# A two-layer fp32 transformer block: which engine empties the banks of interleaved work, and where modulation units of layer 0 stand

## The reference

```python
for layer in range(DEPTH):
    need_ctx = layer < DEPTH - 1
    mod_l = [m[:, None, :] for m in adaln_params(c, w_mod[layer], b_mod[layer])]   # silu(c) @ w_mod + b_mod, in 6
    mod_c = adaln_params(c_ctx, w_mod[layer], b_mod[layer])
    p_l = split_cols(modulate(x, norm1_g[layer], mod_l[0], mod_l[1]) @ w_in[layer])
    p_c = split_cols(modulate(ctx, norm1_g[layer], mod_c[0], mod_c[1]) @ w_in[layer])
    a_l, a_c = diff_attention(...)       # "DA": two softmaxes and their difference
    b_l, b_c = hgrn2_mixer(...)          # "HG": gated recurrence in both directions
    n_l, n_c = neighbourhood_attention(...)
    w_l, w_c = window_gqa(...)
    x = x + mod_l[2] * (jnp.concatenate([a_l, b_l, n_l, w_l], axis=-1) @ w_out[layer])
    x = x + mod_l[5] * squared_relu_mlp(modulate(x, norm2_g[layer], mod_l[3], mod_l[4]), w_ff1[layer], w_ff2[layer])
```

## Time and profile before

| | |
|---|---|
| median of 3 runs | 2276.91 us (2276.86 to 2279.08) |
| the profiled execution | 2280.41 us, its span 2278.6 us |
| mean granted clock of TensorE | 0.959 of full |
| busy, share of the span | TensorE 91%, VectorE 45%, ScalarE 34%, GpSimd 30% |
| DA in layer 0 / layer 1 | 377 to 496 us / 1594 to 1680 us |
| HG's levels in layer 0 / layer 1 | 568.3 to 661.3 us / 1737 to 1805.2 us |

### The profile page before, as it was taken

One profiled execution on the slowest core, in us unless ns is written; L12 is line 12 of the kernel. 1 busy time (PEld: TensorE's weight loads), 2 busy tenths in 40 slices (PEclk: granted clock), 3 DMA queues, 4 the chain that ended last, 5 costly groups with the idle time before them and its releaser, 6 DMA issues.

```text
span 2278.6 us, 32056 instructions
## 1 busy us (share of the span) xinstructions
PE 2083.6 (91%) x13292; PEld 1734.6 (76%) x13292; DVE 1017.8 (45%) x1791; ACT 784.8 (34%) x1283; POOL 686.2 (30%) x567
## 2 busy tenths in 40 slices
PE   5799898889889899999999988998998888999998
PEld 3578787768777788888888867777787677778787
DVE  2535546855775631212213253445857754121122
ACT  1533323434335621312213153233444355232231
POOL 0230212012751232322322323223024513444442
PEclk9889998989999999999999998999999989999999
DMA  8220010342411121121121123010242311222222
GB/s 287 48 74 19 20 38 19 130 138 83 149 57 56 38 74 56 56 75 56 56 74 56 56 46 76 19 38 19 93 119 93 112 56 56 93 93 93 94 91 74
DMA packets 178353, 169.72 MB, mean 74 GB/s; under 512 B 29393, under 2 KB 174753, under 8 KB 178081
## 3 DMA queue, kind: packets, MB, share of 16 engines
q1 hardware_dynamic: 177408, 164.53, 23.4%
q10 hardware_dynamic: 800, 3.15, 0.4%
HBM read 159.79 MB, written 2.10 MB: 71 GB/s over the span
## 4 chain that ended last, share of the span: by engine, by line
PE 75%; DVE 11%; ACT 6%; issue 3%; SPq 2%; DMA 2%; POOL 1%; DVEq 0%; ACTq 0%; POOLq 0%
PE gp L877 52%; PE sp L1109 3%; PE sp L1260 2%; PE gp L1146 2%; PE tp L1126 2%; PE gp L931 1%; SPq L710 1%; PE sp L1100 1%; POOL HGx_kd L775 1%; DVE small L2174 1%; ACT nt L1458 1%; PE sp L950 1%; PE gp L901 1%; PE op L1126 1%; PE op L1146 1%
## 5 line engine op out<-in xcount | busy, mean ns | idle before, releaser
L788 POOL TENSOR_TENSOR wlo<-raw,whi 128x512 fp32r<-128x512 f32 x386 | 514.2, 1365 | 1306.2 <-ACT whi L1424 1306.1
L877 PE MATMUL gp<-xhi,whi 128*128 128x512 f32 (+1 forms) x1424 | 520.5, 366 | 34.8 <-DVE xlo L1963 21.4
L877 PE MATMUL gp<-xhi,wlo 128*128 128x512 f32 (+1 forms) x1424 | 507.3, 356 | 0.0
L877 PE MATMUL gp<-xlo,whi 128*128 128x512 f32 (+1 forms) x1408 | 503.3, 357 | 0.0
L877 PEld LDWEIGHTS gp<-xhi,whi 128*128 128x128 f32 x1424 | 277.0, 195 | 83.2 <-issue 14.5
L1424 ACT ACTIVATE whi<-raw 128x2048 fp32r<-128x2048 f32 (+1 forms) x100 | 187.3, 1874 | 367.9 <-PE gp L877 356.4
L877 PEld LDWEIGHTS gp<-xhi,wlo 128*128 128x128 f32 x1424 | 276.5, 194 | 39.3
L877 PEld LDWEIGHTS gp<-xlo,whi 128*128 128x128 f32 x1408 | 273.7, 194 | 38.6 <-issue 2.0
L877 PE MATMUL gp<-hhi,whi 128*128 128x512 f32 (+1 forms) x768 | 276.4, 360 | 9.6 <-issue 5.0
L877 PE MATMUL gp<-hlo,whi 128*128 128x512 f32 (+1 forms) x768 | 274.9, 358 | 0.0
L877 PE MATMUL gp<-hhi,wlo 128*128 128x512 f32 (+1 forms) x768 | 274.7, 358 | 0.0
(11 more groups left out here) (361 smaller groups left out, 3249.9 us busy)
## 6 DMA issues: line engine op xcount, KB each, us to landing
raw<-in_w_ff SPq DMA_DIRECT2D x64, 1024.0 KB, 5.3
raw<-in_w_mod SPq DMA_DIRECT2D x48, 1024.0 KB, 5.2
raw<-in_w_in SPq DMA_DIRECT2D x20, 1024.0 KB, 5.1
raw<-in_w_in SPq DMA_DIRECT2D x24, 256.0 KB, 4.5
bias<-e SPq DMA_DIRECT2D x96, 32.0 KB
raw<-in_w_out SPq DMA_DIRECT2D x12, 256.0 KB, 3.1
xin<-in_x ACTq DMA_DIRECT2D x1, 2048.0 KB, 9.6
raw<-in_w_out SPq DMA_DIRECT2D x16, 128.0 KB, 3.2
```

Of the source, the lines that this page charges most:

```text
L788: nc.gpsimd.tensor_tensor(wlo[:, s % 2, ks, :], raw[:, index[splits[s]] % 2, ks, :], whi[:, s % 2, ks, :].bitcast(F32), ALU.subtract)\
L877: mm = pe.matmul(out, lhs, rhs, start=(i == 0 and j == 0), stop=(i == KT - 1 and j == 2))
```

## The change

There are two parts. First, ScalarE gets a function `empty`, and VectorE a function `turns`. In DA, and for the modulation rows in HG, ScalarE now copies the banks (row copies in both stages, dense chunks in DA) with its activation instruction; VectorE keeps the turns only. In DA, `empty` stands behind the exponentials of the next slot. In HG it stands behind the second exponential of each pair of levels and, once in a tile, behind `read_out`; it takes slots `level - 4` and `level - 3`. Second, in layer 0 the differential mixer gets 12 modulation units and not 14, HG 12 and not 10, and HG's are spread over eleven twelfths of its slots and not three quarters. Layer 1's plan is as it was.

```diff
@@ fill_plan
-    counts = {("NA", 0): 0, ("SW", 0): 0, ("DA", 0): 14, ("HG", 0): 10, ("NA", 1): 0, ("SW", 1): 0, ("DA", 1): 7, ("HG", 1): 9}
+    counts = {("NA", 0): 0, ("SW", 0): 0, ("DA", 0): 12, ("HG", 0): 12, ("NA", 1): 0, ("SW", 1): 0, ("DA", 1): 7, ("HG", 1): 9}
...
-            span = 3 * n // 4 if m == "HG" else n
+            span = (11 * n // 12 if l == 0 else 3 * n // 4) if m == "HG" else n
@@ scalar
+            def empty(slot):
+
+                for u, c in slot:
+                    if c == "turn":
+                        continue
+                    n = N(u, c)
+                    act.wait_ge(group_done, n + 1)
+                    if c == "row":
+                        dst, src = mrow[:, :], bank(n)[:, 0:UC]
+                    elif c[0] == "tok":
+                        dst, src = buf("HG", "v")[:, c[1], :], bank(n)[:, 0:UC]
+                    else:
+                        a, b = SEGS[c[1]]
+                        dst, src = buf("HG", "q1")[:, c[0], a:b], bank(n)[:, 0:b - a]
+                    nc.scalar.activation(dst, src, ACT.Copy).then_inc(bank_free[group_bank[n]], 1)
...
                     if m == "DA":
                         expo(n + 1)
+                        empty(ENDS[m, l][n])
...
                     if pair == 2 and tt >= 1:
                         read_out(tt - 1)
+                    if level >= 4:
+                        empty(ENDS["HG", l][level - 4])
+                        empty(ENDS["HG", l][level - 3])
                     if level >= 8:
...
                 mix_up()
+                for slot in ENDS["HG", l][6 * ntile - 4:]:
+                    empty(slot)
                 read_out(ntile - 1)
@@ vector
+            def turns(slot):
+
+                fill((u, c) for u, c in slot if c == "turn")
...
-                    fill(EARLY[m, l][n])
-                    finish(n + 1)
-                    fill(ENDS[m, l][n][len(EARLY[m, l][n]):])
+                    if m == "DA":
+                        turns(ENDS[m, l][n])
+                        finish(n + 1)
+                    else:
+                        fill(EARLY[m, l][n])
+                        finish(n + 1)
+                        fill(ENDS[m, l][n][len(EARLY[m, l][n]):])
...
                     if idx >= 1:
-                        fill(ENDS["HG", l][idx - 1])
+                        turns(ENDS["HG", l][idx - 1])
...
-                fill(ENDS["HG", l][-2])
+                turns(ENDS["HG", l][-2])
```

More of the change, by code:

```diff
@@ L1640, in attention @@
                 if m == "DA":
+                    empty(ENDS[m, l][-1])
                     end = LAT if l == DEPTH - 1 else T
@@ L2232, in attention @@
                         copy_turned(n)
-                    fill(EARLY[m, l][n])
-                    finish(n + 1)
-                    fill(ENDS[m, l][n][len(EARLY[m, l][n]):])
+                    if m == "DA":
[5 more added lines that the diff above has]
+                        fill(ENDS[m, l][n][len(EARLY[m, l][n]):])
                     output(n)
-                fill(ENDS[m, l][-1])
+                if m == "DA":
+                    turns(ENDS[m, l][-1])
+                else:
+                    fill(ENDS[m, l][-1])
                 if m == "DA":
@@ L2363, in hgrn @@
                     done += 1
-                fill(ENDS["HG", l][-1])
+                turns(ENDS["HG", l][-1])
                 mix_low(l, MIX_EARLY)
```

## The result

The changed kernel takes 2255.22 us in the median of four runs (2250.81 to 2260.2), the kernel before 2277.99 (2276.86 to 2280.28). The ratio is 0.9896 (95% interval 0.988 to 0.9912): 22.8 us between the medians, where 12.9 were forecast. The range of 2257 to 2272.5 misses it by 1.8 us; the direction was right, the size was not.

The account below looks back on a forecast made before the run. The prediction took TensorE, busy 91% of the span, as the bound, with 41 us idle in the four stretches. Terms of -3.9, -4.1, -3.9 and -1.0 sum to -12.9 us, giving 2264.0 us, range 2257 to 2272.5.

Parts of the forecast that it names:

- term 1: Mixer of layer 0: seven copies off the chain, -2.35 us; two units fewer, -1.5; together -3.9 (-2.4 to -5.3).
- Term 2: Levels of layer 0: TensorE's waits shrink, -6.5 us; two units added, +2.9; idle time filled, -0.5; together -4.1.
- Term 3: Levels of layer 1: waits behind rows go, -4.9 us; two late turns, +1.0; together -3.9 (-2.5 to -4.9).
- Term 4: Mixer of layer 1: three copies off the chain, -1.0 us (-0.3 to -3.0).
- The rival of the two product engines: Levels: GpSimd's and VectorE's products stretch each other and half of the waits come back; 2269.6 us, chance 0.20.
- Its sign: Levels: longer products on both GpSimd and VectorE would show the forecast wrong; no size given.
- The larger gain: Mixer slots held to be set by TensorE shorten too, terms reach their far bounds; 2258 to 2260 us, chance 0.10.
- The slower rival: 21 levels with a row: ScalarE's copy holds up the next exponential, 1.45 us each; 2294 us, chance 0.05.
- The sign: Levels: exponentials starting behind a row copy with no idle time before them would show the forecast wrong; no size given.

Follow-up runs that it names:

- e9: Kernel before, with the row of slot 22 in layer 0's mixer put ahead of the last value chunk; ratio 0.9979.
- e11: Kernel before with the copies moved to ScalarE, old plan, slot 22's row ahead of the chunk and one mixer row computed twice; ratio 0.991.
- e13: Whole change, with the last value chunk of layer 0's mixer whole in slot 22, ahead of the row; 2258.49 us, ratio 0.9912 to kernel before.
- e1: Changed kernel with the old plan (14 and 10 units, three quarters), so only the copies move; ratio 0.9938 to kernel before.
- e4: e1 with the levels' rows emptied by VectorE as before, so only the mixers' copies move; ratio 0.9986 to kernel before.
- e5: e4 with one modulation row of layer 0's mixer computed twice, in TensorE's idle time; ratio 0.9972 to kernel before.
- e2: Kernel before with only the new plan (12 and 12 units, eleven twelfths), copies staying on VectorE; ratio 0.9976.
- e3: e1 with the mixers emptied by VectorE as before, so only the levels' row copies move; ratio 0.9959 to kernel before.
- e6: Whole change run again, unchanged, with a second trace; 2253.67 us, ratio 0.9896 to kernel before.
- e12: Whole change with the last value chunk of layer 0's mixer behind its last slot; ratio 0.9916 to kernel before.
- e7: Whole change without its mixer part: new plan, levels' rows emptied by ScalarE, mixers by VectorE; ratio 0.9934 to kernel before.
- e8: Whole change with 10 and 14 units in layer 0 instead of 12 and 12; ratio 0.9928 to kernel before.

## Why the prediction was wrong

The step that failed is the plan's share of term 1, with the sentence on the end of the mixer: "That row stands in slot 22 of 24 before and after, behind the last value chunk, so these 11.2 us stay as long as they are". The 11.2 us from the request to TensorE's start did stay (10.5). But the number of the slot was compared and not what stands in it. Before, slot 22 holds the whole chunk, 24 matmuls and 2.96 us, ahead of the row. With 12 units the dealing puts 18 of these matmuls into slot 21, and 6 remain ahead of the row. The request moves from 5.3 to 2.5 us behind the last scores. e9 (that alone, in the kernel before: -4.8, interval 2.5 to 7.1) shows it in the time, and all traces in the place of the request; e11 and e13 (taken back, in the changed kernel: +3 to +5) point the same way within their noise. Of the 4.5 us by which the last part of the mixer shortened (24.9 to 20.4) the request is 2.8 and the way from it to TensorE's start 0.7; the rest is for the most part the clock, as the 24 matmuls behind it take 7.61 us where they took 8.52. The prediction gave the plan +0.9 us (-1.5, +2.9, -0.5); it measured -5.5 alone and -9.6 beside the move.

A second cause has no term in the prediction, which treated the clock as noise of 1 to 3 us. In the mixer TensorE's clock falls at some places behind idle time, and each fall in the table of slots costs 1.4 to 2.7 us. With the old plan and the mixer's copies on ScalarE such a fall stands in slot 9 and eats what they win (e1, e4). With the new plan, where slots 9 and 10 are shorter (5.78 to 4.25 and 3.43 to 2.72), it is not there. e5 and e11 speak for the idle time as its cause at that one place, with the rival named at e5 left. The whole change is better than the sum of e2, e3 and e4 by 5.7 us, which is no more than the noise of four such differences; that falls of this kind make it, and the spread of 4 to 16 us between runs of one kernel, is what the traces suggest, not shown: a timed run has no trace.

So the account doesn't close. The two profiled executions are 20.3 us apart, 16.8 of them in the four stages (6.1, 3.6, 2.2 and 4.9) and 3.5 in stretches whose code is the same. The earlier request explains some 5 of the 9.9 us by which the medians beat the forecast; the rest is the terms below and an open part.

Point by point:

- **Term 1, the mixer of layer 0**, -3.9: -6.1 in the first trace and -9.2 in e6. In slots 6 and 11 the copies on the chain give 0.4 and 0.5 us, as read. The sum put the last part of the mixer at nothing, and it gave 4.5 us; up to the last scores the stage gave -1.6 and -4.6.
- **Term 2, the levels of layer 0**, -4.1: -3.6, which comes near by luck. The move gives -6.0 (e1, e3), for which -6.5 stood, but about 2 us are lost again to the slower clock at the start of the levels (0.58 for 0.86). With the clock as before, the levels of the same code take 89.0 to 89.3 us (e13, e12), so the term is -5.5 to -5.8, and the two units take back 0 to 1 us (88.6 to 89.0 in e1, e3 and e11; 89.0 to 89.6 in e12, e13 and e7), not 2.4.
- **Term 3, the levels of layer 1**, -3.9: -4.9 in the trace. Here too the clock of the first 12 us has to be the same on both sides: at 0.57 to 0.64 the levels take 70.0 and 70.3 us with VectorE's copies (before, e9) and 65.1 to 65.6 with ScalarE's (seven traces), at 0.75 to 0.80 they take 68.3 or 68.4 (e2, e4, e5) and 63.9 (e1, e11). That is -4.4 to -4.9 with the same plan. The turn that was to be late by 0.5 us twice was late by 0.5 in all.
- **Term 4, the mixer of layer 1**, -1.0: -2.2, and in all ten traces with the move 97.8 to 98.2 where those without have 100.4 to 103.1. Three pieces were too few; it was sized from one chain.
- **The rival of the two product engines** came in part only. Its sign is there: the mean of both products grew a little in the levels of layer 0, before and after:

```profile
L2331 DVE TENSOR_TENSOR HGx_qd<-HG_q,HG_tmp 128x512 f32<-128x512 f32 x18 | 16.1, 899 | 2.3 <-ACT HG_tmp L1730 2.3
...
L775 POOL TENSOR_TENSOR HGx_kd<-HG_k,HG_tmp 64x256 f32<-64x256 f32 x36 | 33.7, 935 | 16.6 <-ACT HG_tmp L1730 14.6
```

```profile
L2365 DVE TENSOR_TENSOR HGx_qd<-HG_q,HG_tmp 128x512 f32<-128x512 f32 x18 | 16.7, 934 | 3.2 <-ACT HG_tmp L1748 3.2
...
L775 POOL TENSOR_TENSOR HGx_kd<-HG_k,HG_tmp 64x256 f32<-64x256 f32 x36 | 35.8, 995 | 14.4 <-ACT HG_tmp L1748 12.5
```

  With the products from `HGx_exps` (826 to 882 ns, 895 to 932 ns) VectorE's 36 take 1.6 us more and GpSimd's 72 take 3.5. TensorE's wait for the masked copy stayed at 3.6 us where 1 was foreseen, half of what it had been; but the stage is 6 us shorter in e1 with the same wait (3.5), so the rival's price didn't come.
- **The larger gain** was given 0.10 and a floor of 2258, by the mixer's slots alone. It came by another way and went past it.
- **The slower rival**, a copy that holds up the exponentials, did not come, although its sign did: nine exponentials of the two level stretches start behind a row copy with no idle time before them. That of 570.60 does, behind the copy (569.60) and the high half (569.87); TensorE comes to its next scores at 571.63 straight from the row all the same. The sign was badly chosen.

## What to carry to other kernels

When a dealt plan changes, compare what stands ahead of each instruction that releases a transfer, not only its slot: 3 us of dense work put behind one row were worth 4.8 us here (e9), more than the 2.9 us that the two moved units take. Before two stages of different traces are compared, their granted clock should be: the same levels took 91.2 and 89.0 us here, and a faster neighbour can come with a fall of the clock that eats its gain (slot 9 of e1 and e4). A plan's cover for a later load should be looked at again for each count (e8 lost 3.78 us to it).

## What the runs showed of the hardware

TensorE's granted clock went from 1.00 to 0.50 behind gaps of 0.80 and 1.06 us in e4, and stayed at 1.00 in the kernel before, whose gaps there are as long. The busy times of the two in the same windows (0.62 and 1.07 us, 0.97 and 0.63) don't tell the one from the other, so where it falls could not have been read from the trace of before. The slot with the fall took 2.6 us longer. Where the idle time was filled with a second pass of 16 small matmuls (1.93 us for both passes, in e5), the clock stayed and the slot was as short as before; so it was in e11. The first 12 us of the levels of layer 0 had a clock of 0.57 to 0.60 in five of the fifteen traces and of 0.86 to 0.89 in the others; the same code took 2 us longer at the lower one.
